# A streaming hybrid layer on one core: one staging buffer is moved and two loads change their place in SyncE's queue

## The reference, cut to what matters

```python
def _swiglu(x, w_gate, w_up, w_down):
    return (jax.nn.silu(x @ w_gate) * (x @ w_up)) @ w_down      # 1024 -> 2816 -> 1024

    xn = _modulate(_rms(x, g_ffn1), ada[:, 0], ada[:, 1])
    x = x + 0.5 * ada[:, 2][:, None] * _swiglu(xn, w_ffn1_gate, w_ffn1_up, w_ffn1_down)
    ...
    xn = _modulate(_rms(x, g_ffn2), ada[:, 6], ada[:, 7])
    x = x + 0.5 * ada[:, 8][:, None] * _swiglu(xn, w_ffn2_gate, w_ffn2_up, w_ffn2_down)
```

## Time and profile before

| | |
|---|---|
| median of 3 runs | 2400.35 us (2397.86 to 2402.78) |
| profiled execution, its own time | 2396.69 us |
| its span | 2394.8 us |
| TensorE matmul busy | 2340.2 us, 98% |
| VectorE busy | 1579.4 us, 66% |
| ScalarE busy | 984.8 us, 41% |
| GpSimd busy | 129.3 us, 5% |
| queue of SyncE and ScalarE (q1) | 345.15 MB, 41.8% of 16 engines' span |
| granted clock of TensorE, mean | 0.987 |

### The profile page before, as it was taken

How to read it: one execution, slowest core, us unless ns; L and a number is a source line. 1 busy time by engine, 2 the same in 40 slices (tenths; PEclk the granted TensorE clock), 3 DMA queues, 4 the chain that set the end, 5 groups by cost and what they waited for, 6 DMA issues and landing times.

```text
span 2394.8 us, 31657 instructions
## 1 busy us (share of the span) xinstructions
PE 2340.2 (98%) x11530; PEld 2007.1 (84%) x11530; DVE 1579.4 (66%) x2530; ACT 984.8 (41%) x1701; POOL 129.3 (5%) x173
## 2 busy tenths in 40 slices
PE   6999999999999999999999999999999999999998
PEld 4777877787788787999999999997778788878887
DVE  6966665665766766655676565559666567666667
ACT  4544443444333443443344334235444444433335
POOL 0010101100000000101011110000010100000000
PEclk8999999999999999999999999999999999999999
DMA  9465455548855332321222213422644543498642
GB/s 348 159 209 172 163 181 186 167 162 329 310 213 193 130 128 92 118 57 45 66 66 58 63 39 112 149 83 89 219 159 162 193 141 124 151 365 305 237 141 82
DMA packets 247341, 381.01 MB, mean 159 GB/s; under 512 B 16689, under 2 KB 158185, under 8 KB 246070
## 3 DMA queue, kind: packets, MB, share of 16 engines
q1 hardware_dynamic: 234526, 345.15, 41.8%
q0 software_dynamic: 10240, 33.56, 4.5%
q10 hardware_dynamic: 2456, 0.75, 0.1%
HBM read 262.93 MB, written 116.47 MB: 158 GB/s over the span
## 4 chain that ended last, share of the span: by engine, by line
PE 86%; DVE 7%; DMA 3%; issue 2%; ACT 2%; SPq 0%; DVEq 0%; ACTq 0%
PE bank L535 25%; PE bank L537 25%; PE bank L536 25%; PE bank L2933 2%; PE bank L2932 2%; PE bank L2930 2%; PE bank L2816 1%; PE bank L2846 1%; DVE u_lo L629 1%; DMA h_dram<-stage_lo 1%; DMA xrow<-in_x_prompt 1%; DVE x L2265 1%; DMA wraw<-in_w_ffn_up 1%; DVE wraw L656 1%; PE bank L2957 1%
## 5 line engine op out<-in xcount | busy, mean ns | idle before, releaser
L629 DVE TENSOR_TENSOR u_lo<-wraw,u_hi 128x512 fp32r<-128x512 f32 (+2 forms) x532 | 315.1, 618 | 276.6 <-ACT u_hi L623 274.1
L535 PE MATMUL bank<-ops,u_hi 128*128 128x512 f32 x1232 | 489.0, 397 | 8.2 <-DVE ops L1944 4.1
L537 PE MATMUL bank<-ops,u_lo 128*128 128x512 f32 x1232 | 481.9, 391 | 0.0
L536 PE MATMUL bank<-ops,u_hi 128*128 128x512 f32 x1232 | 481.6, 391 | 0.0
L623 ACT ACTIVATE u_hi<-wraw 128x512 fp32r<-128x512 f32 (+2 forms) x532 | 287.5, 568 | 279.1 <-PE bank L537 174.5
L535 PE MATMUL bank<-xn_hi,w_hi 128*128 128x384 f32 x1104 | 370.6, 336 | 5.2 <-ACT ww L1691 2.0
L536 PE MATMUL bank<-xn_lo,w_hi 128*128 128x384 f32 x1104 | 369.7, 335 | 0.0
L537 PE MATMUL bank<-xn_hi,w_lo 128*128 128x384 f32 x1104 | 369.5, 335 | 0.0
L535 PEld LDWEIGHTS bank<-ops,u_hi 128*128 128x128 f32 x1232 | 232.7, 189 | 85.1 <-issue 23.5
L537 PEld LDWEIGHTS bank<-ops,u_lo 128*128 128x128 f32 x1232 | 232.4, 189 | 49.7
L536 PEld LDWEIGHTS bank<-ops,u_hi 128*128 128x128 f32 x1232 | 232.7, 189 | 46.3
(11 more groups left out here) (320 smaller groups left out, 3957.1 us busy)
## 6 DMA issues: line engine op xcount, KB each, us to landing
h_dram<-stage_hi SPq DMA_DIRECT2D x154, 256.0 KB, 2.4
h_dram<-stage_lo SPq DMA_DIRECT2D x154, 256.0 KB, 2.7
ada_in<-in_w_ada POOLq DMA_DIRECT2D x96, 256.0 KB, 3.7
raw<-in_w_in SPq DMA_DIRECT2D x48, 512.0 KB, 4.7
wraw<-in_w_ffn_gate SPq DMA_DIRECT2D x44, 512.0 KB, 5.0
wraw<-in_w_ffn_up SPq DMA_DIRECT2D x44, 512.0 KB, 5.0
wraw<-in_w_ffn_down SPq DMA_DIRECT2D x48, 384.0 KB, 4.8
x<-x_dram SPq DMA_DIRECT2D x6, 2304.0 KB, 9.0
```

What stands on the lines that cost most here:

```text
L535: nc.tensor.matmul(out, hi, mov_hi, start=first, stop=False, skip_group_check=True)
L536: nc.tensor.matmul(out, hi, mov_lo, start=False, stop=False, skip_group_check=True)
L537: return nc.tensor.matmul(out, lo, mov_hi, start=False, stop=last, skip_group_check=True)
L629: nc.vector.tensor_tensor(unit(u_lo, f, g, u, n), unit_source(u, n), unit(u_hi, f, g, u, n).bitcast(F32), ALU.subtract).then_inc(u_lo_read ...
```

## The change

`h21` goes from (6, 0) to (0, 1), inside slot H, and `stage_hi0` from (0, 1) to (6, 0), where `hs_in1` comes later. The load of slot H no longer has to wait for the stores of stages 0, 3 and 6 nor for those of 2 and 5. It waits for those of stages 1 and 4, and stands behind the store of stage 6 and ahead of w01 and w11. What waits for the other stores is now `load_samples(1)`, behind w01 and w11. The load of slot E (O_T3) goes from ahead of the store of stage 3 to behind it. The same code runs in both networks. No arithmetic is changed, and as many bytes are moved.

```diff
-        ("g22", (0, 0)), ("g21", (1, 0)), ("h22", (2, 0)), ("h21", (6, 0))))
+        ("g22", (0, 0)), ("g21", (1, 0)), ("h22", (2, 0)), ("h21", (0, 1))))
     g12, h12 = over_x("g12", 1, 1), over_x("h12", 3, 1)
-    stage_hi = [over_x("stage_hi0", 0, 1, F32R), over_x("stage_hi1", 2, 1, F32R), over_x("stage_hi2", 4, 0, F32R)]
+    stage_hi = [over_x("stage_hi0", 6, 0, F32R), over_x("stage_hi1", 2, 1, F32R), over_x("stage_hi2", 4, 0, F32R)]
...
                 load_slot(f, 0, 3)
                 store_samples(f, g)
                 store_stage(f, g, 2)
+                store_stage(f, g, 3)
                 load_slot(f, 0, 4)
-                store_stage(f, g, 3)
                 store_stage(f, g, 4)
                 store_stage(f, g, 5)
                 after(E_P3[1])
...
                 next_weights(f, g + 1, 0, 0)
                 next_weights(f, g + 1, 1, 0)
                 store_stage(f, g, 6)
+
+                count = f * ROUNDS + ROUNDS
+                sp.wait_ge(stage_stored[1], 32 * count * 2)
+                load_slot(f, 0, 6)
                 next_weights(f, g + 1, 0, 1)
                 next_weights(f, g + 1, 1, 1)
-                count = f * ROUNDS + ROUNDS
-                for s in range(3):
-                    sp.wait_ge(stage_stored[s], 32 * count * (3 if s == 0 else 2))
+                sp.wait_ge(stage_stored[0], 32 * count * 3)
+                sp.wait_ge(stage_stored[2], 32 * count * 2)
                 sp.wait_ge(hs_stored, 32 * count)
-                load_slot(f, 0, 6)
                 load_samples(1)
```

## The result

| | before | after |
|---|---|---|
| median | 2400.57 us (20 runs, 2397.85 to 2405.17) | 2404.03 us (20 runs, 2400.47 to 2408.85) |
| ratio of the times, 95% interval | | 1.0017 (1.001 to 1.0023) |
| profiled execution: own time, span | 2396.69, 2394.8 us | 2400.70, 2399.2 us |
| first pass to second pass, first network | 39.15 us | 40.69 us |
| first pass to second pass, second network | 38.18 us | 40.94 us |

The changed kernel is 0.17% slower, about 4 us. The interval leaves out 1, so it is slower, but by less than the 0.2% which the prediction took for what can be told from no change. Forecast were 2401.8 us, range 2396.0 to 2406.0. Measured are 2404.03.

What follows compares the result with a forecast made beforehand. TensorE, busy for 98% of the span, was taken to bound the kernel. First network -0.7 and second +2.2 us, together +1.5, added to the median 2400.35 gave 2401.8 us, range 2396.0 to 2406.0.

Steps and rivals of the forecast that it cites:

- d: Delay of w11 and so VectorE's second sum: 2.2 us in both networks; shifts next pass d - 2.9 and d.
- rival 3: Slower: hold-up of the whole load or more, d from 3.9, TensorE's path up to 1 us longer; 2406 us, chance 0.10.
- Step 1: Slot E behind stage 3's store: removes waits of 1.13 and 1.56 us ahead of slot D, stage 6 3.8 us earlier.
- Step 2: Stage 6's store and w00, w10, issued earlier, stand right behind slot F and fill the queue at 602 to 603 us.
- the hole: Partly idle DMA queue at 602 to 603 us, DMA share 0.24; filling it gives the weights 1.6 us per network.
- Step 3: Slot H ahead of w01 and w11: the 3.18 us wait for H goes, VectorE's sums begin 2.2 us later.
- Step 4: Behind w01, w11: TensorE waits 3.0 us at A22's second tile; VectorE's chain puts next pass 9.2 us after second sum.
- The clock: TensorE's granted clock of 0.50 behind its wait for slot H, costing 1.7 us, swallowed by the wait for VectorE's chain.
- Rival 1: w01, w11 not held up by slot H, d from -1 to +0.8; 2397.4 us at d = 0, chance 0.18.
- Rival 2: All meant gains come true, copy and VectorE's chain having slack: -6.0 and at least -1.9 us, 2392.5 us; chance 0.07.
- Rival 4: Stage 6 stays late, held by something other than stage 3's store: d = 3.8, +4.7 us, 2405 us; chance 0.05.

Runs made afterwards that it cites:

- fifth alone: On the kernel before, only slot E's load put behind stage 3's store, slot H's load left behind all stores and the weights; ratio 1.000.
- seventh alone: On the changed kernel, slot E's load put back ahead of stage 3's store; ratio 1.0032, median 2407.53 us.
- pair after F: On weights first, SyncE waits for slot F's landing before it issues w00 and w10; one execution, 2404.95 us.
- weights first: On the changed kernel, w01 and w11 put back ahead of slot H's load; ratio 0.9986, 2397.96 us.
- third ahead: On the changed kernel, slot H's load split, 512 KB ahead of w01 and w11 and 1024 KB behind them; ratio 1.0003.
- fifth split: On weights first, slot E's load split, 512 KB ahead of stage 3's store and the rest behind it; ratio 0.9994.
- x updates ahead: On weights first, VectorE's two updates of x for the next pass put ahead of units 2 and 3 and sums 5 and 6; ratio 0.9968, 2392.85 us.
- copy ahead: On the changed kernel, ScalarE's copy for A22's second tile put ahead of unit 4 of the next pass; ratio 1.0028.
- fifth split, pair after F: On fifth split, SyncE waits for slot F's landing before it issues w00 and w10; one execution, 2404.73 us.

## Why the prediction was right, and what it mis-sized

**Right by the bound, 2.8 us low in the sum.** The forecast was +1.5 us; the two stretches show +4.30. The mechanism held, and one term was mis-sized: d, for which 2.2 was taken in both networks, is 4.3 in the first and 2.8 in the second (31.33 less 27.04, 31.70 less 28.93). Put into the prediction's own formula, d - 2.9 gives +1.4 (measured +1.54) and +d gives +2.8 (measured +2.76). The mean of the two, 3.5, lies outside the 0.8 to 3.3 that the prediction gave its forecast, and below the 3.9 of rival 3. The time is inside the range because the range went up to d = 3.8, not because 2.2 was near.

**Step 1.** Stage 6 was forecast at 593.0 and comes at 593.35; both waits ahead of slot D are gone. The sentence that failed is "So E costs nothing". The cover named for it was that slot E lands before 605.1. It does, at 589.57 + 8.5 = 598.1. But the cost lay elsewhere: slot F was taken to stay at 603.0 since nothing ahead of it grew, and it lands at 605.2. The queue's rate was taken as constant; it fell when slot E's bytes were no longer waiting in it. The experiments show that slot F is late with slot E's late issue and not for what follows it (fifth alone 21.40, seventh alone 20.01, pair after F 22.03), and the 812 KB that the queue moves less account for the 2.0 us. Why the rate falls is open. In the second network slot F is not late (21.94 before, 21.92 after).

**Step 2, the hole.** It was to give 1.6 us to the weights in each network. The fifth alone shows 0.0 and 1.33: what the filled hole gives in the first network is lost again through slot F.

**Step 3, slot H ahead of the weights.** Slot H was forecast in time, and TensorE doesn't wait for it any more. Its landing, 612.4, isn't the forecast 610.3, but S4 begins only at 619.35. The price of slot H for the weights, forecast at 3.8 us, is 3.88 and 3.96 us by the experiment that undoes it. The other term of d, the 1.6 us of the hole, is what was mis-sized: against before, the second sum of weights first gains 1.19 us in the second network and loses 0.41 in the first. 3.88 + 0.41 and 3.96 - 1.19 are the 4.3 and 2.8 of d. The order in which the prediction let things land behind slot F holds: it had 9.5 us from slot F to w11, and the second sum at 614.80 is 9.6 after slot F. This is also the measured side of what the prediction drew from the Trainium skill, "DMA: Bandwidth & Descriptors", section "Queues, rings and completion order": 3.9 to 4.0 us for 1536 KB, 1.3 for 512 KB (both counted from slot F's landing), and nothing for what is queued behind (slot F without its followers). The traces agree with it.

**Step 4.** The new wait ahead of A22's second tile was forecast at 3.0 us and is 3.71 and 2.91. A22's first tile, which waits 1.22 us for the copy behind stage 6's store, wasn't foreseen: the store lands at 608.6, not at 606.5. It costs nothing, as the second tile's wait ends later anyway. That none of these waits sets the next pass is confirmed by the copy moved ahead: the wait goes, the next pass comes no sooner. The 9.2 us from the second sum to the next pass hold in all kernels with the old order of VectorE whose TensorE isn't late for another reason:

| kernel | second sum, second network | next pass | between |
|---|---|---|---|
| after | 2152.76 | 2162.00 | 9.24 |
| fifth alone | 2145.13 | 2154.38 | 9.25 |
| seventh alone | 2157.72 | 2166.97 | 9.25 |
| weights first | 2145.36 | 2154.60 | 9.24 |
| third ahead | 2148.25 | 2157.49 | 9.24 |
| fifth split | 2148.97 | 2158.21 | 9.24 |

**The clock.** At 618 to 619 us the changed kernel has a granted clock of 0.50 too, as before. The prediction let this be swallowed by VectorE's chain; in the first network it just is: TensorE begins the next pass without a wait, 9.36 us after the second sum. Its own path from A22's second tile to the next pass takes 8.81 us (615.35 to 624.16), where the prediction had 6.1 + 1.7 = 7.8: behind the wait the granted clock is 0.50 for 5.4 us, where behind the 3.18 us, from which the 1.7 were taken, it was so for 3.4.

**The rivals.** Rival 1 (weights not held up) falls with the second sums at 614.80 and 2152.76. Rival 2 (all comes true) falls with the next pass; 2392.5 us is what the kernel reaches only after weights first and the x updates ahead. Rival 3 (slower) came close. Its condition, d from 3.9 on, and its sign, sums after 614, are met in the first network; in the second the condition is not, and its extra cost of a TensorE path longer than VectorE's didn't appear beyond 0.1 us. It stood at 2406, the forecast at 2401.8, and the time came between them. Rival 4 was excluded by stage 6 at 593.35, and the seventh alone shows what it would have cost.

**What the change is worth in its parts.** Slot E behind the store, with the two buffers exchanged and the weights first: -3.7 us in the two stretches (ratio 0.9986). Slot E behind the store alone is already -4.2 us, so the exchange of the buffers, which lets slot H go earlier, gained nothing more here. Slot H ahead of the weights: +8.0 us in the two stretches. The change put a good half and a bad half together.

## What to carry to other kernels

When a load is put ahead of another in a full queue, price the one behind it by the bytes of the one ahead (here 3.9 us for 1536 KB), and look for which of the two has slack: slot H could land 2 us late here, the weights not at all. Follow the wait that is removed to the chain that ends just behind it (VectorE's 9.2 us), before the largest wait in the profile is taken for the cost. A load that goes back in the queue "for free" can be needed there as filling, and then the transfer behind it lands late, so look at the rate in windows of 1 us and not at the load's own deadline alone.

## What the runs showed of the hardware that was not expected

**A rate that falls while the engines count as busy.** At 593 to 594 us the changed kernel has a DMA share of 1.12 and moves 188 GB/s, where 397 went at a share of 1.03 before. A busy share near 1 doesn't say that a queue moves what it could. The mechanism in the DMA engines wasn't tested.

**The end of a transfer.** In "pair after F" nothing stands behind slot F, and its end can be seen by itself:

```profile
604.80:605.00 0.20, 0.20 (x2) 0.17 (x1) 0.20 (x1) 0.00 (x0) 0.00 (x0) 1.00 0.05 20
605.00:605.20 0.20, 0.20 (x2) 0.19 (x1) 0.20 (x2) 0.00 (x0) 0.00 (x0) 1.00 0.05 20
605.20:605.40 0.20, 0.20 (x2) 0.17 (x1) 0.20 (x2) 0.00 (x0) 0.00 (x0) 1.00 0.00 0
```

A share of 0.05 is about one of the 16 engines, so in its last 0.6 us (from 604.6 on) the load is down to about one engine. From 605.2 on nothing moves, and the landing is counted at 605.73, 0.5 us behind the last bytes. The next load, issued at 605.71, moves its first bytes between 606.6 and 606.8, 0.9 to 1.1 us behind its issue. The Trainium skill, "DMA: Bandwidth & Descriptors", section "Anatomy of one DMA", gives a fixed 2.0 us for setup and completion together, most of it behind the last byte, for loads issued by GpSimd; for these, issued by SyncE, the trace shows about 1.5 us together, and the smaller part behind the last byte. The prediction let slot F's bytes end before 602 by that page. In the kernel before the queue still moves 41 GB/s at 602.2 to 602.4 us and 5 GB/s at 602.4 to 602.6, with slot F's landing at 603.03, so they end at about 602.5, and its estimate that d falls by 0.5 us for it is not borne out.

**The clock and the waits.** TensorE's granted clock was 0.50 behind idle times of 3.71 and 2.91 us (changed kernel), 3.18 us (before) and 4.63 us (copy ahead, 619 to 622 us), but 1.00 behind waits of 2.37 us (seventh alone, 2158 to 2160 us) and 2.43 us (fifth split, pair after F, at 2152 us). In the changed kernel's first network it was 0.50 until about 620.8, 5.4 us past the end of the wait; no run here tells why it lasted longer there than in the second.
